# Late gathers behind the last down weights, and two reordered stretches between the layers of a hybrid SSD/attention/MoE block

## What is computed

```python
        a_l = modulate(x_lat, norm1_g[layer], sh1, sc1)
        a_c = modulate(x_ctx, norm1_g[layer], csh1, csc1)
        ...
            y = hier_moe(jnp.concatenate([f_l, f_c], axis=0), *moe_args)
            x_lat = x_lat + g2 * y[: b * n_lat].reshape(b, n_lat, d)
            x_ctx = x_ctx + cg2 * y[b * n_lat:].reshape(b, n_ctx, d)
...
    def run_block(args):
        xblk, e = args
        return (jax.nn.silu(xblk @ w_gate[e]) * (xblk @ w_up[e])) @ w_down[e]
```

## Time and profile before

| | us |
|---|---|
| median of 3 runs | 1724.24 |
| lowest, highest | 1722.67, 1729.59 |
| the profiled execution | 1721.01 |
| its span in the profile | 1719.2 |

### The profile page before, as it was taken

How to read it: one execution, slowest core, us unless ns; L and a number is a source line. 1 busy time by engine, 2 the same in 40 slices (tenths; PEclk the granted TensorE clock), 3 DMA queues, 4 the chain that set the end, 5 groups by cost and what they waited for, 6 DMA issues and landing times.

```text
span 1719.2 us, 21680 instructions
## 1 busy us (share of the span) xinstructions
PE 1541.8 (90%) x8536; PEld 788.1 (46%) x8536; DVE 621.5 (36%) x1314; ACT 373.7 (22%) x766; POOL 214.5 (12%) x233
## 2 busy tenths in 40 slices
PE   5999999999999899999787788899999998788786
PEld 3434444455444454545344444345565554344343
DVE  2534347888633315312111112748422211111112
ACT  2311147898510100000000000228110000000000
POOL 2000002222110011011001012111001011001001
PEclk9999999999999899999999999999999999999999
DMA  9687668933489699999999999832699999999996
GB/s 373 240 324 276 264 221 209 330 130 127 148 297 281 243 381 425 425 424 425 427 427 427 427 426 418 335 155 71 224 368 423 415 425 426 426 427 425 427 426 255
DMA packets 144656, 572.67 MB, mean 333 GB/s; under 512 B 22939, under 2 KB 79787, under 8 KB 113728
## 3 DMA queue, kind: packets, MB, share of 16 engines
q1 hardware_dynamic: 123888, 524.98, 76.4%
q0 software_dynamic: 14640, 26.03, 4.3%
q10 hardware_dynamic: 6048, 20.58, 3.5%
HBM read 543.01 MB, written 49.25 MB: 344 GB/s over the span
## 4 chain that ended last, share of the span: by engine, by line
PE 56%; DMA 34%; DVE 6%; issue 2%; ACT 1%; SPq 0%; POOL 0%; ACTq 0%; DVEq 0%; POOLq 0%
DMA mem<-in_moe_w_down_dram 18%; PE bank L2066 13%; DMA mem<-in_moe_w_gate_dram 12%; PE bank L640 9%; PE bank L2081 7%; PE bank L1007 6%; PE bank L952 4%; PE bank L2528 3%; PE bank L376 2%; DMA consts<-in_consts_dram 2%; PE bank L2635 2%; PE bank L974 1%; DVE mem L1183 1%; PE bank L2052 1%; PE bank L985 1%
## 5 line engine op out<-in xcount | busy, mean ns | idle before, releaser
L2066 PE MATMUL bank<-mem 128*64 128x256 f32 x4096 | 495.6, 393 | 65.0 <-DMA mem<-in_moe_w_gate_dram 39.0
L2066 PEld LDWEIGHTS bank<-mem 128*64 128x64 f32 x4096 | 284.6, 135 | 273.4 <-DMA mem<-in_moe_w_gate_dram 61.1
L2081 PE MATMUL bank<-mem 128*64 128x512 f32 x1040 | 243.1, 610 | 45.0 <-DMA mem<-in_moe_w_down_dram 41.1
L640 PE MATMUL bank<-mem 128*128 128x512 f32 x384 | 171.2, 598 | 1.2 <-DMA mem<-in_ssd_w_in_dram 1.2
L2263 ACT ACTIVATE mem<-bank 128x256 f32<-128x256 f32 x65 | 25.0, 384 | 668.5 <-PE bank L2066 645.7
L2003 POOL DMA_INDIRECT ys_dram<-mem x61 | 61.2, 1004 | 747.6 <-DVE mem L2345 713.3
L2081 PEld LDWEIGHTS bank<-mem 128*64 128x64 f32 x1040 | 72.2, 139 | 176.1 <-issue 122.2
L2345 DVE TENSOR_TENSOR mem<-bank,mem 128x512 f32<-128x512 f32 x65 | 44.9, 691 | 233.3 <-PE bank L2081 183.3
L2324 DVE TENSOR_TENSOR mem<-mem,bank 128x256 f32<-128x256 f32 x65 | 27.4, 421 | 263.6 <-PE bank L2066 155.7
L640 PEld LDWEIGHTS bank<-mem 128*128 128x128 f32 x384 | 70.8, 190 | 97.9 <-issue 95.8
L952 PE MATMUL bank<-mem 128*128 128x512 f32 x256 | 115.2, 592 | 0.0
(11 more groups left out here) (357 smaller groups left out, 1510.3 us busy)
## 6 DMA issues: line engine op xcount, KB each, us to landing
mem<-in_moe_w_up_dram SPq DMA_DIRECT2D x61, 2048.0 KB, 20.3
mem<-in_moe_w_gate_dram SPq DMA_DIRECT2D x61, 2048.0 KB, 26.4
mem<-in_moe_w_down_dram SPq DMA_DIRECT2D x60, 2048.0 KB, 15.0
mem<-in_mod_w_dram SPq DMA_DIRECT2D x24, 2048.0 KB, 14.4
ys_dram<-consts SPq DMA_DIRECT2D x55, 512.0 KB, 7.5
mem<-in_ssd_w_in_dram SPq DMA_DIRECT2D x10, 2048.0 KB
mem<-ac_dram ACTq DMA_DIRECT2D x32, 512.0 KB, 4.5
mem<-in_ssd_w_out_dram SPq DMA_DIRECT2D x4, 2048.0 KB
```

Source lines behind the costliest of these rows:

```text
L640: mm = nc.tensor.matmul(psum[c % 2][:, :], lhsT=w[:, k, (c % 4) * P:(c % 4 + 1) * P], rhs=aT[0][:, k, :], start=(k == 0), stop=(k == KD - 1))
L2066: mm = nc.tensor.matmul(bank[half * BR:(half + 1) * BR, 0:HF], lhsT=x[:, k], rhs=w[k][:, half::2], start=(k == 0), stop=(k == KD - 1), ski ...
L2081: mm = nc.tensor.matmul(bank[half * BR:(half + 1) * BR, :], lhsT=ht[:, k // 2, k % 2 * BR:(k % 2 + 1) * BR], rhs=w[:, k, half * COLS:(half ...
```

## The change

POOL gathers only the first tiles at once (two in layer 0, one in layer 1) and waits for `tail_in[2]` before the gathers of the others. In layer 0, DVE does `norm1_cols_dve` and `combine_dve` of tile 1 ahead of `gated` of the last block. The `late_add_dve` of tiles 2 and 3 are cut into halves that stand between the steps of the norm. PE starts the first query product after groups 0 and 1 of the copied transposes and takes its chunks 4 to 7 after groups 2 and 3.

```diff
+        EARLY_TILES = [2, 1]
...
             for t in range(nt):
+                if t == EARLY_TILES[l]:
+                    pool.wait_ge(tail_in[2], 16 * (l + 1))
                 for k, buf in enumerate(cy):
                     pool.indirect_dma_start(buf[:, t, :], None, ys_dram[l],
...
                 if j == a + 1:
                     combine_dve(dve, l, 0)
+                    if l == 0:
+                        norm1_cols_dve(dve)
+                        combine_dve(dve, l, 1)
                 gated(j)
-            combine_dve(dve, l, 1)
-            for t in range((3, 2)[l]):
+            if l:
+                combine_dve(dve, l, 1)
+            for t in range(2):
                 late_add_dve(dve, l, t)
...
             stream_turn_pe(pe, 0)
+            unit_wait(pe, U_QKV)
+            pe.wait_ge(n1_ea, 5)
+            pe.wait_ge(n1_ed, 5)
+            project(0, 0, 0, range(4))
             pe.wait_ge(n1_ea, 6)
             pe.wait_ge(n1_ed, 6)
-            unit_wait(pe, U_QKV)
-            project(0, 0, 0)
+            project(0, 0, 0, range(4, KD))
             project(0, 1, 1)
...
-            norm1_cols_dve(dve)
             stream_mean_dve(dve, 0)
+            late_add_dve(dve, 0, 2, [0])
             stream_rows_dve(dve, 0)
-            late_add_dve(dve, 0, 3)
+            late_add_dve(dve, 0, 2, [1])
+            late_add_dve(dve, 0, 3, [0])
             stream_evac_dve(dve, 0)
+            late_add_dve(dve, 0, 3, [1])
             combine_dve(dve, 0, 2)
```

More of the change, by code:

```diff
@@ L2434, in combine_dve, with late_add_dve @@
                 ins.then_inc(cb_x, 1)
-        def late_add_dve(dve, l, t):
+        def late_add_dve(dve, l, t, halves=(0, 1)):
             dve.wait_ge(cb_mm, base_t[l] + t + 1)
-            for half in range(2):
+            for half in halves:
                 x = xin[:, t, half * COLS:(half + 1) * COLS]
```

## The result

| | us |
|---|---|
| before, median of 12 | 1724.36 |
| changed kernel, median of 12 | 1728.14 (1726.10 to 1731.62) |
| ratio, with its 95% interval | 1.0022 (1.0012 to 1.0032) |
| profiled execution, its span | 1727.70, 1725.8 |

The changed kernel is 3.8 us slower. That is inside the half per cent called "no change" ahead of the run, but the interval lies wholly above 1, the forecast of 1722.2 had the wrong sign, and the time is above the range that ended at 1727.5.

The account below looks back on a forecast made before the run. The prediction took DMA to bound most of both MoE stages, with PE and DVE work between. Gains of 1.7 us at the seam and 0.3 at layer 1's end made 2.0 off the median 1724.24: 1722.2, range 1717.0 to 1727.5.

Parts of the forecast that it names:

- The clock: PE's clock at the first query product: no loss in the forecast case; a rival added 1.7 us for a lower clock.
- forecast case: Whole kernel: 2.0 us faster, 1722.2 against the median, with 1719.5 to 1724.5 given a chance of 0.50.
- late gathers: Rival, both layers: L of 7.2 us loses 2.4, giving 1726.6, or 1728.3 with the lower clock; chance 0.18.
- POOL's issue: Layer 0's four deferred gathers: one issued every 1.25 us, from the release at 1075.9 to the last at 1079.8.
- L: Time the last deferred gather takes to land on an emptied queue: taken as 5.0 us, between 2.2 and 7.2.
- The release: End of POOL's wait in layer 0, when the last down weights land: 1075.9, between 1074.2 and 1076.6 (no gain).
- the seam: Between layers 0 and 1, up to the first query product: 1.7 us gained, with PE starting at 1093.4.
- layer 1: End of layer 1: weights released at 1704.7 instead of 1707.0, tile 1's gathers landing at 1711.1, 0.3 us gained.
- The weights gain nothing: Rival, both layers: releases stay at 1076.6 and 1707.0, seam gains 1.0, end loses 2.1, giving 1725.3; chance 0.12.
- Quick gathers: Rival, both layers: a gather lands in about 2.5 us or less, gaining 6.5 us, giving 1717.7; chance 0.20.
- the seam does not carry: Rival: something other than the attention stage holds layer 1's DMA stream, the 1.7 is lost: 1723.9; no separate chance.
- DVE's new order: Layer 0: `gated` 1.6 us earlier and the norm's rows at 1087.0, 3.3 us earlier than 1090.29.

Follow-up runs that it names:

- e1: The kernel before with POOL's waits for the last down weights alone, in both layers, without DVE's new order: 1727.39, ratio 1.0018 to the kernel before.
- e7: The changed kernel with 14 products of constants on PE between the transposes and the wait for `w_qkv`: 1726.39, ratio 1.0014 to the kernel before.
- e3: The changed kernel with POOL's early wait in layer 0 only: 1726.85, ratio 1.0015 to the kernel before.
- e12: The changed kernel with all gathers behind POOL's wait in both layers: 1727.21 in one execution, beside 1726.13 before.
- e2: The changed kernel without POOL's early waits, keeping DVE's new order and the halved query product: 1723.16, ratio 0.9988 to the kernel before.
- e4: The changed kernel with POOL's early wait in layer 1 only: 1721.70, ratio 0.9985 to the kernel before.
- e8: As e2, with SP holding the `w_qkv` and `w_o` loads back for no gather: 1723.77, ratio 0.9992 to the kernel before.
- e5: The changed kernel, both POOL waits kept, with SP holding `w_qkv` only for the gathers of tiles 0 and 1: 1722.52, ratio 0.9987 to the kernel before.

## Why the prediction was wrong, point by point

**The mechanism was found, its sign was not.** The prediction named what decides: the transfer of `w_qkv` behind the late gathers takes the place of the operands. The trace shows just that. It put the unit at 1093.3; it came at 1097.86. Of these 4.6 us 1.6 are drift: P was at 1059.04 before and is at 1060.61 in the new trace. From P the forecast had the first query product at 34.4 us, and it came at 37.3. These 2.9 us and the clock are what failed, term by term:

- *The clock, in the forecast case at nothing, measured 1.7.* This is the largest single step that failed. The prediction puts an idle time of "some 2.8 us" into its rival of late gathers. But from its own numbers 2.8 is the idle time of the forecast case (1093.4 less 1090.6); the rival's would be about 5. The forecast case had more idle time than the 1.94 us that had lowered the clock at 1076.62, and still ran the product at full speed. It idled 4.23 and took 15.70 for 13.97; e1's 2.33 us cost the same 1.7, and e7 took the 1.7 away by filling the idle time.
- *POOL's issue, from the release to the last gather: forecast 3.9, measured 5.2.* The 1.25 us for each came from gathers that run while DVE is mostly idle. The late ones run beside DVE's additions and take 1.79, 1.17, 1.02 and 0.94.
- *L, forecast 5.0, measured 6.0* (6.09 in e1, 5.79 in e3). It was between the bounds of 2.2 and 7.2, 1.0 too low. By the figure of the Trainium skill quoted in the prediction it would have been 3.2; the runs do not bear that out for the last of four gathers in a row, even with the engines nearly empty. The first gather of e12, issued with no other under way, took 4.4.
- *The release, forecast 0.6 us sooner than before, measured no sooner.* The weights landed 17.45 us after P in both traces. The range came from bytes: four gathers away are 1.0 MB less ahead of the weights, 2.4 us. The bytes were counted rightly, but the fifth to eighth gather cost the weights nothing. The witness at hand was better than it looked: by the issue of the load, layer 1 with four gathers waited 29.55 us against 27.79; counted from P it is 17.57 against 17.58.

With these the prediction's own sum reads 1078.1 + 0.3 + 4.9 + 6.0 + 8.5 = 1097.8, which is the trace. Over the whole kernel, the seam was to gain 1.7 and lost 2.9, and layer 1 was to gain 0.3 and lost 1.0: 5.9 us in sum. The forecast of 1722.2 and the measured median of 1728.14 are 5.9 us apart.

**The rivals.** "Late gathers" with the clock gave 1728.3, and the median is 1728.14. The number is right by errors that cancel, which is luck: it took the landing for 7.2 us, 1.2 too long, with the release 0.6 too early and POOL's issue 1.3 too short. "The weights gain nothing" was true of layer 0, but by itself gave 1725.3, since it kept the full clock and the short issue times. "Quick gathers" and "the seam does not carry" are refuted by 6.00 and by 576.95 against 577.6.

**What held.** DVE's new order and the halves together: the reordered kernel without waits (e2, e4) has the seam 2.2 to 3.2 us shorter from P, though its `gated` stands behind the addition. From the end of `gated` to the mean the forecast was 4.7 us and the trace has 4.9. The halves of the query product bring nothing in the changed kernel, as said. The seam's change is carried on one for one. For layer 1 the weights were forecast 2.3 us earlier and are 2.1 earlier. The end still lost 1.0 us in place of 0.3 gained, since POOL's two issues and the last landing took 1.1 longer than forecast. Over all traces the wait of layer 1 is about even: from P to tile 1's addition it is 22.7 to 23.2 us with it, and without it 23.3 to 23.9 where the last down product took 4.99 to 5.35 us (e2, e3, e8) and 21.9 where it took 3.65 (before). With the wait PE idles only some 0.66 us there, and the product took 3.65 in all seven traces.

**The chances.** Half of the weight lay on a case in which three estimates, each chosen inside its bounds, all had to hold and the clock had to stay up. The release and the landing were not chosen rashly (near the late end, and just above the middle of 2.2 and 7.2), but all three fell short in the same direction, and the clock came on top. "Within 0.5%" came true, the range did not.

## What to carry to other kernels

Before a transfer is put off until a weight load is in, follow what is queued behind it on every engine: here one wait on POOL held SP's next 2 MB load, which cost some 3.5 us of PE's time and then its clock. Bytes taken off the DMA engines do not speed a load by their amount: here the first four gathers cost the last load 1 us each and the next four nothing, so see in a run which of them count. Count from an event near the load on the same path; from its issue, the effect of two gathers was hidden under 2 us of scatter. And where a load waits for several buffers to come free, wait for those alone whose space it takes or whose data the next step needs, and fill an unavoidable wait of PE with products on constants.

## What the runs showed of the hardware

- **The slow end of a load.** In e12, with no gather under way, the DMA share was 0.53 in 1070:1072, 0.16 in 1072:1074 and 0.05 after; the load landed at 1074.7. Most of its bytes were in some 2.5 us earlier.

```profile
1070.00:1072.00 2.00, 2.00 (x18) 1.21 (x18) 0.00 (x0) 0.31 (x2) 0.00 (x0) 1.00 0.53 221
1072.00:1074.00 2.00, 2.00 (x20) 1.06 (x16) 0.00 (x0) 0.00 (x0) 0.00 (x0) 1.00 0.16 66
```

- **Idle time and the clock.** Idle times of 1.83 to 2.02 us ahead of the last down product of layer 0 were followed by 4.98 to 5.35 us for it in eight traces, but by 3.65 in two (1.92 us in e2, 1.91 in e5; the changed kernel's 1.87 gave 4.98). Ahead of the down product at about 1037 to 1040, 1.82 to 1.85 us were followed by 3.65 in all of ten traces. Idle times of 2.33, 3.97 and 4.23 us ahead of the first query product lowered the clock in all three. Which way a wait of 1.9 us goes is not settled by its length.
- **A gather's issue beside DVE.** The first late gather took 1.79 us on POOL here (1.80 in e1, 1.70 in layer 1), each while DVE did a `combine_dve` from SBUF (L2436). In e12, after a still longer wait of POOL, it took 1.15 in layer 0 with DVE on shorter work, and 0.99 in layer 1 with DVE waiting:

```profile
1074.97 1.15 POOL L2038 DMA_INDIRECT mem<-ys_dram,mem  x1 [23.67 <-DMA mem<-in_moe_w_down_dram]
...
1707.74 0.99 POOL L2038 DMA_INDIRECT mem<-ys_dram,mem  x1 [23.34 <-DMA mem<-in_moe_w_down_dram]
```

The Trainium skill, page "GPSIMD Engine Reference", section "Key points", says that POOL shares its SBUF interfaces with VectorE and contends with operations that have two SBUF inputs; L2436 is one. The traces agree, and e12 says that the idle time before is not the reason. But the second late gather of the changed kernel, also beside L2436, took only 1.17, so the length is not explained.
